# Second attention of a fused two-layer kernel: softmax units in pairs, the first two pairs' scores among the projections, one scaling of two on GpSimd

## The reference, cut to what matters

```python
# second layer, 256 latent tokens x, 256 context tokens; h and hc are normed and modulated
# window attention: 8 query heads of 64 in 2 groups of 4 that share a key head
s = einsum(q, concat(k_context, k_band)) * 64 ** -0.5 + band_bias
p = softmax(concat(s, sink))[..., :-1];  o_a = p @ v          # a sink logit a head
# latent (MLA) attention: 8 heads, keys of 64 + 32
s = (qn @ kn + qr @ kr) * 96 ** -0.5
p = softmax(s);  o_b = p @ v
x = x + g_a * (concat(o_a, o_b) @ w_out)
h2 = modulate(rmsnorm(x))
x = x + g_f * ec_moe(h2, w_router, w_gate, w_up, w_down)      # 16 experts, 32 tokens each
return rmsnorm(x)
```

## Time and profile before

| | us |
|---|---|
| three runs | 704.82, 705.34, 707.81 |
| median | 705.34 |
| profiled execution, its own time | 705.55 |
| its span in the profile | 703.7 |
| PE busy | 596.1 (85%) |
| DVE busy | 295.1 (42%) |
| ACT busy | 224.1 (32%) |
| POOL busy | 17.6 (3%) |
| TensorE clock granted, mean | 0.946 of full speed |

### The profile page before, as it was taken

One profiled execution on the slowest core, in us unless ns is written; L12 is line 12 of the kernel. 1 busy time (PEld: TensorE's weight loads), 2 busy tenths in 40 slices (PEclk: granted clock), 3 DMA queues, 4 the chain that ended last, 5 costly groups with the idle time before them and its releaser, 6 DMA issues.

```text
span 703.7 us, 8506 instructions
## 1 busy us (share of the span) xinstructions
PE 596.1 (85%) x3351; PEld 367.7 (52%) x3351; DVE 295.1 (42%) x725; ACT 224.1 (32%) x483; POOL 17.6 (3%) x34
## 2 busy tenths in 40 slices
PE   6989999999998979979998999977995775665663
PEld 6978886878676757648654444436430321221010
DVE  3365676666574252464728876145110100010005
ACT  4344454435344224365235666111010100010001
POOL 3000000000000001000000000000000000000000
PEclk9999999999999999999999999997998979898687
DMA  8595756777686790354475002754999999999992
GB/s 335 208 360 192 279 206 261 285 277 294 266 327 271 272 406 39 119 210 180 169 305 243 0 1 73 286 206 183 375 430 427 426 424 431 428 424 427 426 414 85
DMA packets 19080, 193.00 MB, mean 274 GB/s; under 512 B 3296, under 2 KB 4576, under 8 KB 7264
## 3 DMA queue, kind: packets, MB, share of 16 engines
q1 hardware_dynamic: 15584, 188.49, 66.6%
q10 hardware_dynamic: 3168, 2.39, 1.1%
q0 software_dynamic: 288, 1.57, 0.5%
HBM read 190.87 MB, written 1.05 MB: 273 GB/s over the span
## 4 chain that ended last, share of the span: by engine, by line
PE 63%; DMA 24%; DVE 7%; ACT 3%; issue 2%; POOL 0%; SPq 0%; ACTq 0%; POOLq 0%; DVEq 0%
PE bank L1017 25%; DMA qk<-in_stream 17%; PE bank L994 5%; PE bank L1005 5%; DMA ring<-in_stream 5%; PE bank L1523 3%; PE bank L1436 3%; PE bank L1282 3%; PE bank L1399 3%; PE bank L1367 2%; PE bank L1056 2%; PE bank L1364 2%; PE bank L1470 2%; PE bank L1309 2%; DMA vvc<-vvc 1%
## 5 line engine op out<-in xcount | busy, mean ns | idle before, releaser
L1017 PE MATMUL bank<-weight_parts,u_parts 128*128 128x512 f32 (+2 forms) x416 | 126.7, 387 | 3.7 <-ACT rows L654 1.2
L1752 DVE TENSOR_TENSOR weight_parts<-ring,weight_parts 128x1024 fp32r<-128x1024 f32 (+2 forms) x64 | 73.3, 1180 | 46.1 <-ACT weight_parts L654 44.0
L1017 PEld LDWEIGHTS bank<-weight_parts,u_parts 128*128 128x128 f32 x416 | 76.5, 190 | 21.2 <-issue 2.1
L654 ACT ACTIVATE weight_parts<-ring 128x1024 fp32r<-128x1024 f32 (+2 forms) x64 | 64.1, 1022 | 33.6 <-PE bank L1017 24.0
L1017 PE MATMUL bank<-weight_parts,x_parts 128*128 128x512 f32 (+1 forms) x128 | 48.3, 378 | 0.0
L994 PEld LDWEIGHTS bank<-ident,sp 128*128 128x128 f32 (+1 forms) x218 | 26.1, 140 | 24.8 <-DVE sp L2040 15.6
L1017 PE MATMUL bank<-u_parts,weight_parts 128*128 128x256 f32 x192 | 36.7, 288 | 2.2 <-DVE weight_parts L1752 2.2
L994 PE MATMUL bank<-ident,sp 128*128 128x128 f32 (+1 forms) x218 | 32.1, 274 | 3.5 <-DVE sp L2040 1.9
L705 ACT ACTIVATE sp<-sp,small 128x128 f32<-128x128 f32 (+1 forms) x48 | 21.3, 444 | 35.8 <-DVE small L1713 35.8
L1017 PEld LDWEIGHTS bank<-u_parts,weight_parts 128*128 128x128 f32 x192 | 30.4, 191 | 3.3 <-issue 2.2
L2145 DVE SCALAR_TENSOR_TENSOR sp<-sp,bank 128x512 f32<-128x512 f32 x4 | 2.8, 688 | 60.3 <-ACT sp L924 60.3
(11 more groups left out here) (292 smaller groups left out, 1032.6 us busy)
## 6 DMA issues: line engine op xcount, KB each, us to landing
ring<-in_stream SPq DMA_DIRECT2D x44, 2048.0 KB, 9.3
parts<-in_stream SPq DMA_DIRECT2D x12, 2048.0 KB, 35.0
qk<-in_stream SPq DMA_DIRECT2D x10, 2048.0 KB, 13.0
tabs<-in_stream SPq DMA_DIRECT2D x5, 2048.0 KB, 35.5
mo<-in_stream SPq DMA_DIRECT2D x5, 2048.0 KB, 38.7
vvc<-in_stream SPq DMA_DIRECT2D x5, 2048.0 KB, 37.6
tz<-in_stream SPq DMA_DIRECT2D x5, 1024.0 KB, 39.6
lat<-in_stream SPq DMA_DIRECT2D x5, 1024.0 KB, 41.7
```

The lines of the kernel that those rows point to most:

```text
L654: ins = act.activation(dst, src, ACT.Copy, scale=scale)
L1017: ins = pe_.matmul(o, lhs(a, c, i), rhs(b, c, i), start=(c == 0 and n == 0), stop=(c == chunks - 1 and n == 2))
L1752: dve.tensor_tensor(quarter(weight_parts[:, SLOT:], name, q), quarter(slot(name), name, q), quarter(weight_parts, name, q).bitcast(F32), A ...
```

## The change

The units go in 16 pairs s, unit 2s and 2s + 1. What moves:

- A window pair is now one query half of one head from each of the two groups (`unit_of`), and its two products run in the upper and the lower 64 rows of the array (`tile_position`), on unpadded keys `kwin` (one DVE copy for two, and no GpSimd zeros).
- Scores have four banks (3, 4, 0, 1) and exponentials four tiles (`soft_at`), for three.
- Pairs 0 and 1 are taken into `SCHEDULE`: scores, maxima and exponentials of pair 0 behind `qu11`, reciprocals of pair 0 and scores, maxima and exponentials of pair 1 behind `xkv11`, reciprocals of pair 1 behind `kx3`. The loops begin at pair 2.
- GpSimd scales the even unit of a pair (128 x 512, 16 instructions), DVE the odd one.
- DVE now does both maxima of a pair and then both reciprocals of the same pair; before, it did the reciprocal of the unit before between two maxima. It copies every fourth window unit's transposes (every second before) and every odd latent unit's (none before).
- PE does two key tiles of the values product at once; `ou00` and `ou01` are both begun among the last units.

```diff
+        if name == "qu11":
+            out.append(("pair", 0))
+        if name == "xkv11":
+            out += [("weigh", 0), ("pair", 1)]
+        if name == "kx3":
+            out.append(("weigh", 1))
...
-        kP = view(vv, 0, 1024, "p (g s) -> p g s", g=2)
+        kwin = view(vv, 0, 512)
...
-        sp3 = sp[:, :].rearrange("p (u k) -> p u k", u=3)
+        soft_at = [view(modr, 1024, 512), view(pt, 1024, 512), view(sp, 0, 512), view(sp, 512, 512)]
...
+        S4 = (bank[3], bank[4], bank[0], bank[1])
+        def score_bank(u):
+            s = u // 2
+            return S4[(2 * (s - 1) if s else 0) % 4 + u % 2]
...
+        def unit_of(u):
+            if u < 16:
+                return u // 4, u % 2, u // 2 % 2
+            return (u - 16) // 4, u // 2 % 2, u % 2
         def vector_turns(u):
-            return u < 16 and u % 2 == 1
+            return u % 4 == 3 if u < 16 else u % 2 == 1
...
+            def soften(u):
+                eng.wait_ge(u_neg, u + 1)
+                if u < 16:
+                    act.activation(soft_at[u % 4], soft_at[u % 4], ACT.Exp, bias=nm2[:, u:u + 1],
+                                   accum_out=sm2[:, u:u + 1]).then_inc(u_exp, 1)
+                    j, b, _ = unit_of(u)
+                    h = 4 * b + j
+                    act.activation(sk2[:, u:u + 1], sink[:, h:h + 1], ACT.Exp, bias=nm2[:, u:u + 1]).then_inc(u_sink, 1)
+                else:
+                    eng.wait_ge(u_turn, u - 3)
+                    act.activation(soft_at[u % 4], score_bank(u)[:, :], ACT.Exp, bias=nm2[:, u:u + 1], scale=MLA_SCALE,
+                                   accum_out=sm2[:, u:u + 1]).then_inc(u_exp, 1)
...
+                elif kind == "pair":
+                    soften(2 * n)
+                    soften(2 * n + 1)
...
+            def finished(p):
+                eng.wait_ge(u_pv, p + 1)
+                copy(oT[:, p, :], OB[p % 2][:, 0:S]).then_inc(u_out, 1)
+            for s in range(2, 17):
+                if s == 2:
+                    for u in range(2):
+                        unit_turned(eng, u, copy).then_inc(u_turned_a, 1)
+                if s < 16:
+                    soften(2 * s)
+                    soften(2 * s + 1)
+                if s >= 4 and s % 2 == 0:
+                    finished((s - 4) // 2)
+                for u in (2 * s - 2, 2 * s - 1):
+                    if not vector_turns(u):
+                        unit_turned(eng, u, copy).then_inc(u_turned_a, 1)
+            finished(7)
...
+                if n == 10:
+                    for u in range(0, 32, 2):
+                        eng.wait_ge(u_recip, u + 1)
+                        pool.tensor_scalar(soft_at[u % 4], soft_at[u % 4], rc2[:, u:u + 1], None, ALU.mult)\
+                            .then_inc(u_norm_even, 1)
...
-                    pool.memset(vv[:, 0:1024], 0.0).then_inc(kp_zeroed, 1)
...
+            def scores_free(s):
+                if s == 1:
+                    eng.wait_ge(u_masked, 2)
+                if s == 2:
+                    for x in ("kx2", "kx3"):
+                        kept(eng, x)
+                if s >= 3:
+                    eng.wait_ge(u_masked, 2 * s - 2)
+                if s >= 10:
+                    eng.wait_ge(u_exp, 2 * s - 2)
+            def window_scores(s):
+                if s == 0:
+                    for x in ("qwT0", "qwT1", "kwT"):
+                        kept(eng, x)
+                    eng.wait_ge(masked, len(UNITS))
+                scores_free(s)
+                for b in range(2):
+                    j, _, q = unit_of(2 * s)
+                    h = slice(HD * b, HD * b + HD)
+                    pe_.matmul(score_bank(2 * s + b)[:, :], qwT[h, j, q * P:(q + 1) * P], kwin[h, :], start=True, stop=True,
+                               tile_position=(HD * b, 0)).then_inc(u_scores, 1)
...
+                scores_free(s)
+                for u in (2 * s, 2 * s + 1):
+                    h, q = (u - 16) // 2, u % 2
+                    pe_.matmul(score_bank(u)[:, :], qmT[0:QK, h, q * P:(q + 1) * P], kmT[0:QK, h, :], start=True, stop=True)\
+                       .then_inc(u_scores, 1)
...
-                eng.wait_ge(u_norm, u + 1)
+                eng.wait_ge((u_norm_even, u_norm)[u % 2], u // 2 + 1)
...
-                w = weights("OUT0", KC, 512)
+                    arrived(eng, f"OUT{h}")
+                    eng.wait_ge(u_exp, 30)
+                    begin(name)
...
+            for s in range(2, 17):
+                if s == 2:
+                    unit_turn(0)
+                    unit_turn(1)
+                if s < 8:
+                    window_scores(s)
+                elif s < 16:
+                    latent_scores(s)
+                if s >= 3:
+                    first_tile = 0 if s % 2 else 2
+                    pair_pv((s - 3) // 2, range(first_tile, first_tile + 2))
+                if s == 16:
+                    first_output(0, 0, 4)
+                unit_turn(2 * s - 2)
+                unit_turn(2 * s - 1)
+            first_output(0, 4, 6)
+            pair_pv(7, range(4))
+            first_output(1, 0, 6)
+            first_output(0, 6, KC)
+            first_output(1, 6, KC)
...
+            def unit_max(u):
+                _, _, q = unit_of(u)
+                eng.wait_ge(u_scores, u + 1)
+                if u == 0:
+                    eng.wait_ge(wmask_in, 16)
+                if u < 16:
+                    if u >= 4:
+                        eng.wait_ge(u_turn, u - 3)
+                    ins = dve.tensor_tensor_reduce(soft_at[u % 4], score_bank(u)[:, :], wB[:, q, :], 1.0, -3e38, ALU.add,
+                                                   ALU.max, mx2[:, u:u + 1])
+                else:
+                    ins = dve.tensor_reduce(mx2[:, u:u + 1], score_bank(u)[:, :], AX_X, ALU.max)
+                ins.then_inc(u_masked, 1)
+            def unit_neg(u):
+                eng.wait_ge(u_masked, u + 1)
+                if u < 16:
+                    j, b, _ = unit_of(u)
+                    h = 4 * b + j
+                    ins = dve.tensor_scalar(nm2[:, u:u + 1], mx2[:, u:u + 1], sink[:, h:h + 1], -1.0, ALU.max, ALU.mult)
+                else:
+                    ins = dve.tensor_scalar(nm2[:, u:u + 1], mx2[:, u:u + 1], -MLA_SCALE, None, ALU.mult)
+                ins.then_inc(u_neg, 1)
+            def unit_sum(u):
+                eng.wait_ge(u_exp, u + 1)
+                if u < 16:
+                    eng.wait_ge(u_sink, u + 1)
+                    dve.tensor_tensor(sm2[:, u:u + 1], sm2[:, u:u + 1], sk2[:, u:u + 1], ALU.add).then_inc(u_summed, 1)
+            def unit_recip(u):
+                unit_sum(u)
+                if u < 16:
+                    eng.wait_ge(u_summed, u + 1)
+                dve.reciprocal(rc2[:, u:u + 1], sm2[:, u:u + 1]).then_inc(u_recip, 1)
+                if u % 2:
+                    eng.wait_ge(u_recip, u + 1)
+                    dve.tensor_scalar(soft_at[u % 4], soft_at[u % 4], rc2[:, u:u + 1], None, ALU.mult).then_inc(u_norm, 1)
...
+                elif kind == "pair":
+                    for u in (2 * n, 2 * n + 1):
+                        unit_max(u)
+                        unit_neg(u)
+                elif kind == "weigh":
+                    unit_recip(2 * n)
+                    unit_recip(2 * n + 1)
...
-                        eng.wait_ge(kp_zeroed, 1)
-                        leave(spread_keys(name, D_(name)[:, :], kP), name)
+                        leave(dve.tensor_copy(kwin, D_(name)[:, :]), name)
...
+            for s in range(2, 17):
+                if s < 16:
+                    for u in (2 * s, 2 * s + 1):
+                        unit_max(u)
+                        unit_neg(u)
+                    unit_recip(2 * s)
+                if vector_turns(2 * s - 1):
+                    unit_turned(eng, 2 * s - 1, dve.tensor_copy).then_inc(u_turned_v, 1)
+                if s < 16:
+                    unit_recip(2 * s + 1)
```

128 lines of the change are left out of this document (16 added, 112 removed).

## The result

The changed kernel takes 701.86 us (median of 13 runs, 700.73 to 705.39), the kernel before, run beside it, 706.43 (13 runs): a ratio of 0.9949, interval 0.9935 to 0.9964. The forecast of 701.2 was close in part by luck: what it expected up to the latent part was 3.2 us too much, and what it expected behind that 2.2 too little, and the two nearly cancelled.

What follows compares the result with a forecast made beforehand. The end hangs on when the first expert products begin, with PE's attention bounding the path there. Gains of 3.7 up to the latent units and 0.8 in latent pairs, less 0.2, make 4.3 off 705.55: 701.2 us, range 700.0 to 705.0.

Steps and rivals of the forecast that it cites:

- The bound and the exchange rate: Experts' weight stream: its restart hangs on the first expert products, so a us saved ahead of them is saved at the end.
- The rival without gain at the end: Between 454 and 491 us, waits might grow by what was saved: time 705; chance 0.08.
- Pairs 0 and 1 among the projections: Projections: copies delayed, kx3's by 3.6 us, yet the maximum of unit 4 comes 1.8 us earlier net.
- Score products side by side: Window part on PE: a pair's two score products overlap whole, 0.98 us in place of 1.93.
- the rival without overlap: Window part: row products don't overlap, PE's pair is 4.05 us, gain about 2.4, time 703.2; chance 0.07.
- DVE's chain of 3.8: Window part: DVE becomes the bound at 3.8 us a pair, against 4.15 on PE; six pairs take 22.9.
- GpSimd's scaling: Scaling of a pair's even unit on GpSimd: estimated 0.83 us, bounds 0.52 and 1.3, hidden from PE.
- DVE waits for GpSimd: Window part: DVE's sum waits for GpSimd's scaling, W of 0.83 to 1.1; time 703.2 to 704.8; chance 0.27.
- the slower rival: Window pairs: GpSimd takes over 1.5 us and holds DVE; with W = 2.0 time 711 to 713; chance 0.08.
- Latent pairs: Latent part: PE stays the bound at 4.05 us a pair, 0.1 cheaper in each of 8 pairs, 0.8 together.
- Eight now follow each other: 1.06 for 1.17. That is 0.1 less a pair: PE's values products by two tiles: eight instructions in a row take 1.06 us, not 1.17, 0.1 less a pair.
- The drain: Behind the last scores: ou00's residual work delays ou01's by about 0.8 us, covered by ou10's 16 products on PE.

Runs made afterwards that it cites:

- e11: e10 plus 14 unread products on PE ahead of the router's second transposes; 698.1 us, ratio 0.9885 to the kernel before.
- e6: e1 with the four units of pairs 0 and 1 spread in single pieces among the projections; ratio 0.9901 to the kernel before.
- e10: e5 and e6 together: DVE scales every unit, ACT copies all window transposes, pairs 0 and 1 spread out; 699.08 us, ratio 0.9900.
- e5: e1 with ACT also making the window part's copies of transposes that DVE made; ratio 0.9926 to the kernel before.
- e7: e1 with GpSimd doing a same-size instruction into memory nobody reads, where it had scaled the even window units; ratio 0.9985 to the kernel before.
- e2: Changed kernel with pairs 0 and 1 issued after the last projection, not among the projections; ratio 1.0011 to the kernel before.
- e8: Changed kernel with both score products of a window pair on the same 64 rows of the array; ratio 0.9950 to the kernel before.
- e1: Changed kernel with DVE scaling both units of every pair and GpSimd none; 699.87 us, ratio 0.9915 to the kernel before.
- e3: Changed kernel with PE's latent part issued one unit's product of each kind in turn instead of two together; 713.44 us, ratio 1.0117.
- e9: e1 with PE's latent part issued singly in turn, the same edit as e3; 708.2 us, ratio 1.0033 to the kernel before.

## Why the prediction came out as it did

**The bound and the exchange rate** were right: 3.3 us earlier at the first expert product gave 3.3 at the end of the trace, in e11 9.1 gave 9.0 (8.1 by the ratio). The rival without gain at the end is out for this kernel, though e6 and e10 show that up to 2 us can be lost in the stretch that it named.

**Pairs 0 and 1 among the projections.** The queue was followed rightly: the copy of `xkv10` is 2.6 later (forecast 2.6), that of `qm0` 4.6 (4.3). The step that failed is "I take 4.5" from there to `kx3`: 5.75. Without the fall of the clock it is 4.6, in e5 and e7. The price list of the earlier trace rows held only PE without standstill; the prediction saw that `qm0`'s copy was 4.3 late and didn't ask what PE does meanwhile. From `kx3` to the maximum of unit 4 it took 1.96, forecast 2.0. The gain at this mark was 0.3 where 1.8 was forecast. Still, e2 shows that without the move nothing is gained: it is worth 3.1.

**Score products side by side**: 1.05, forecast 0.98, with full overlap. Right in size and without value here, since the next bound, at 4.29, was above PE's old 4.15. For the same reason the rival without overlap had its price wrong: it took 1.9 us off the gain, and e8, which has no overlap, is as fast.

**DVE's chain of 3.8** is right as a sum of DVE's and ACT's own parts (3.77 in e5), where even DVE's scaling of both units fits in. But the prediction put it down for a kernel in which GpSimd works. The pair there is 2.53 + 1.56 + 0.28, less 0.09 by which the next maximum starts before the scaling ends: 4.28. Over the five pairs from maximum 4 to maximum 14 it costs 2.4. PE was then ready for the latent scores 1.3 behind maximum 14 (402.50 to 403.81), where the prediction had taken 2.0, which gives 0.7 back.

**GpSimd's scaling**: 1.57, above the upper bound of 1.3. The step that failed is the price by element taken from a fill, which reads nothing. The bound "at half the pace" had no row behind it.

**The rival "DVE waits for GpSimd"** (0.27) described what happened in the window part, except that its W of 0.83 to 1.1 was too small and that the scaling is held to GpSimd's end and not the sum. That the time fell to the forecast and not to this rival's 703.2 to 704.8 is luck: the latent pairs made up for it. It and the slower rival, which was to lose from a W of 1.5 on, added 0.4 to 0.8 behind GpSimd; it is 0.19. With it the pair of 4.15 is reached from W = 1.43 on, and the loss is 0.14 a pair, not 0.4.

**Latent pairs**: 3.76 on PE (412.00 to 415.76) against 4.05 forecast. The step that failed is "Eight now follow each other: 1.06 for 1.17. That is 0.1 less a pair". The break of 0.11 was read correctly from the earlier trace rows, but it was counted for the values products alone, though scores and transposes are joined too. Three such breaks are 0.4 a pair, 3.1 in eight; the wait of 0.60 for ACT's copy in the second pair takes a part of it back, and the stage gained 2.4 in place of 0.8.

**The drain.** From the end of the latent part to the experts 0.4 more was gained, where the prediction had taken off 0.2 for small delays. Of the 0.4, 0.25 lies behind the router's first transposes (30.09 before, 29.84 after), where traces of the same code differ by 2, so that part can't be put down to the change. The cover by `ou10` held: PE's next row there begins without an idle time.

So 3.2 too much in the projections and the window part (1.5 and 2.4, less 0.7), 1.6 too little in the latent part and 0.6 in the drain: 4.3 forecast, 3.3 in the traces, 3.6 by the runs. The range of 700.0 to 705.0 held, with two of its main terms wrong.

## What to carry to other kernels

Work that is given to GpSimd beside a busy DVE has two prices, its own latency and what DVE can't do meanwhile; if DVE has gaps of the size of the work, leave it on DVE. Issuing products of one kind together, at two units instead of one, saved a tenth of PE's time here, without any change of the arithmetic. And when work is moved into another stage, put it in single pieces between the copies that the stage's next step needs: whole pairs brought 3.1 us, pieces 1.6 more at the router (e10 against e5), and 2.5 where the whole pairs had also cost a fall of the clock (e6 against e1).

## What the runs showed of the hardware

**GpSimd's scaling of 128 x 512 fp32 by a column** takes 1.56 to 1.57 us in 15 of 16 cases and 1.68 in one, beside a DVE that works; that is three times DVE's 0.49. In e7 all eight took 1.86, each with a scaling of DVE begun 0.06 ahead; whether this or the other operand is the reason, no run separates. The Trainium skill, "GPSIMD Engine Reference", section "3.1 Elementwise — side-by-side cycle accounting", has 0.77 for 512 elements in a good loop; this instruction takes twice that.

**The hold is not for a whole instruction.** In the changed kernel the scalings of DVE that were issued 0.93 to 1.34 behind the start of GpSimd's all seem to begin at 1.36, so that they end 0.28 behind its end. One that was issued 0.22 behind its start took 0.75 and ended well before GpSimd did. The small sum with two operands, issued 0.44 behind it, took 0.26 in place of 0.16. And in one case in the changed kernel and all of e3's latent part, where the scaling was issued 0.74 and 0.88 behind the start, it took 0.49 and GpSimd 1.68 and 1.83:

```profile
417.44 1.83 POOL L993 TENSOR_SCALAR modr<-modr,small 128x512 f32<-128x512 f32 x1 [3.43 <-DVE small L1839]
...
418.32 0.49 DVE L1842 TENSOR_SCALAR pt<-pt,small 128x512 f32<-128x512 f32 x1
```

In these cases GpSimd's instruction came first and DVE's ran in the middle of it unhindered. The Trainium skill, in the section named above on who interferes with whom, has the lock last the whole instruction; here the measured 0.49 decides. The cases fit an instruction that holds the ports in two stretches, up to about 0.5 and from about 0.9 to 1.36, and leaves them free between. The stretches are inferred from the durations, and no run was made to test them.

**The granted clock after a standstill of PE.** After the same 2.4 us it fell in e1 and e9 and not in e5, at a cost of 0.9 between e1 and e5. Within the window part of e1 it fell to 0.53 behind a standstill of 1.76. Behind the longer one of 3.69 ahead of the router's second transposes it was between 0.50 and 0.63 in the next 5.5 us in all thirteen traces with that gap, and where it rose again differed: the way from there to the experts took 17.25 to 19.26 us for the same code, with 1.6 of the difference in the last gather. One profiled execution is therefore not good enough to compare two kernels to a us behind such a place.
